# Attention scores in two full passes and packed remainders, in pairs of steps

## The reference

```python
s = (jnp.einsum('bqhd,bkhd->bhqk', q_blk[..., :QK_NOPE], k_nope)
     + jnp.einsum('bqhr,bkr->bhqk', q_blk[..., QK_NOPE:], kpe))
p = jax.nn.softmax(s.astype(jnp.float32) * scale, axis=-1).astype(v.dtype)
return jnp.einsum('bhqk,bkhd->bqhd', p, v)
```

## Time and profile before

| | us |
|---|---|
| median of three runs (3669.15 to 3674.01) | 3669.3 |
| the profiled execution, its own time | 3676.24 |
| its span, all instructions | 3674.5 |
| TensorE busy (17218 matmuls) | 3212.6, 87% |
| VectorE busy | 2016.3, 55% |
| ScalarE busy | 1054.0, 29% |
| GpSimd busy | 1035.4, 28% |

### The profile page before, as it was taken

The page is one execution under the profiler, slowest core; times in us unless marked ns, Lnnn a source line. Parts: engine busy times, 40 slices in busy tenths (PEclk is TensorE's granted clock), DMA queues, the critical chain, the costliest instruction groups (busy, mean ns, idle before and its releaser), DMA issues. The chain is left out here.

```text
span 3674.5 us, 44483 instructions
## 1 busy us (share of the span) xinstructions
PE 3212.6 (87%) x17218; PEld 2521.2 (69%) x17218; DVE 2016.3 (55%) x2246; ACT 1054.0 (29%) x1410; POOL 1035.4 (28%) x619
## 2 busy tenths in 40 slices
PE   8999999993969999999999958979982899999991
PEld 7788888871436666666666636678871789999991
DVE  2427557475357566666667644444448455555553
ACT  3411111112333333333333331212320333333332
POOL 0000000002003233333333342213320765555551
PEclk9999999995989999999999988999985899999995
DMA  4313122122230100100010025455420566666656
GB/s 169 112 39 125 57 88 99 65 99 72 71 84 20 23 5 21 23 23 5 21 23 5 6 86 166 140 194 196 140 96 27 180 195 191 189 189 189 191 162 224
DMA packets 131647, 368.44 MB, mean 100 GB/s; under 512 B 17616, under 2 KB 41952, under 8 KB 120832
## 3 DMA queue, kind: packets, MB, share of 16 engines
q1 hardware_dynamic: 89248, 259.69, 22.0%
q0 software_dynamic: 22080, 73.51, 7.2%
q10 hardware_dynamic: 20160, 33.04, 2.4%
HBM read 263.17 MB, written 102.91 MB: 100 GB/s over the span
## 5 line engine op out<-in xcount | busy, mean ns | idle before, releaser
L1057 DVE TENSOR_REDUCE at_mpart<-at_mx 128x4 f32<-128x1024 f32 (+1 forms) x291 | 352.5, 1211 | 319.1 <-PE at_mx L998 318.1
L931 ACT ACTIVATE at_w<-at_sc 128x1024 f32<-128x1024 f32 (+1 forms) x296 | 298.6, 1011 | 675.5 <-PE at_sc L978 675.5
L957 POOL TENSOR_TENSOR at_part<-at_part,at_w 128x512 f32<-128x512 f32 x224 | 291.2, 1300 | 449.4 <-ACT at_w L931 448.5
L1862 POOL TENSOR_TENSOR moe_gu_lo<-moe_raw_gu,moe_gu_hi 128x2048 fp32r<-128x2048 f32 x64 | 297.8, 4659 | 134.8 <-ACT moe_gu_hi L1901 134.4
L1010 PE MATMUL at_acc<-at_w,V 128*64 128x256 f32 (+1 forms) x2368 | 326.3, 397 | 0.0
L492 DVE SCALAR_TENSOR_TENSOR fr_r<-fr_r,fr_dw 128x2334 f32<-128x2334 f32 x120 | 318.0, 2650 | 3.9
L367 PE MATMUL fr_po<-hT_hi,fr_w_hi 128*128 128x512 f32 (+1 forms) x800 | 297.2, 371 | 2.1 <-PE fr_tp L367 1.2
L367 PE MATMUL fr_po<-hT_hi,fr_w_lo 128*128 128x512 f32 (+1 forms) x800 | 294.7, 368 | 0.0
L367 PE MATMUL fr_po<-hT_lo,fr_w_hi 128*128 128x512 f32 (+1 forms) x800 | 294.7, 368 | 0.0
L976 PE MATMUL at_sc<-at_q_hi,at_k_hi 97*128 97x512 f32 (+1 forms) x592 | 264.2, 446 | 0.0
L1979 DVE TENSOR_TENSOR moe_d_lo<-moe_raw_d,moe_d_hi 128x1024 fp32r<-128x1024 f32 x64 | 190.1, 2971 | 107.7 <-ACT moe_d_hi L1922 107.7
(11 more groups left out here) (316 smaller groups left out, 6961.0 us busy)
## 6 DMA issues: line engine op xcount, KB each, us to landing
moe_raw_gu<-w_gate_up SPq DMA_DIRECT2D x64, 1024.0 KB, 5.8
moe_raw_d<-w_down SPq DMA_DIRECT2D x64, 512.0 KB, 3.9
fr_wm<-w_ada_rows POOLq DMA_DIRECT2D x32, 512.0 KB, 4.7
gates_scratch<-fr_r ACTq DMA_DIRECT2D x64, 256.0 KB, 2.0
mx_gates<-gates_scratch SPq DMA_DIRECT2D x64, 256.0 KB, 4.0
fr_raw<-w_in SPq DMA_DIRECT2D x28, 512.0 KB, 4.4
fr_r<-x POOLq DMA_DIRECT2D x18, 512.0 KB, 4.7
op_m_raw<-mixed_scratch SPq DMA_DIRECT2D x9, 1024.0 KB, 5.9
```

What stands on the lines that cost most here:

```text
L931: act.activation(w[:, g % NW, :, 0:n], sc[:, 2 * (g % 2):2 * (g % 2) + 2, 0:n], ACT.Exp, scale=SM_SCALE).then_inc(exp_done, 1)
L957: pool.tensor_tensor(part[:, j % 2, 1, 0:n], before, w[:, g % NW, 1, 0:n], ALU.add).then_inc(add_p, 1)
L1057: dve.tensor_reduce(mpart[:, 0:q, c], max_bank(m)[:, 0:q, :], AX.X, ALU.max).then_inc(red_done, 1)
L1862: pool.tensor_tensor(gu_lo[:, slot], raw_gu[:, slot], gu_hi[:, slot].bitcast(F32), ALU.subtract).then_inc(glo_done, 1)
```

## The change

Scores. A key tile's 96 + 96 + 96 rows and the row of maxima are 289; the new layout packs them into two passes of 128 rows and 33 rows of rest. `ka`/`qa` hold hi·hi and the first 32 rows of lo·hi; `kb`/`qb` the other 64 rows of lo·hi and the first 64 of hi·lo; `kr`/`qr` the last 32 of hi·lo and the maximum row. In `kr` even key tiles lie in partitions 0 to 32 and odd ones in 64 to 96, and `qr` holds its rows twice, so that the rests of the two tiles of a step are products in two row halves of the array.

Order. Steps are taken in pairs. On TensorE: the rests of both steps (`rests`), the scores of g, the maximum products of g + 11, the scores of g + 1, the maximum products of g + 12, the values of g - 2 and of g - 1. A turn comes before the rests, or before the values with the maximum products behind them. On VectorE: reduction of g + 11, adds of g - 2 and g - 1, reduction of g + 12, splits.

Splits. Two lo instructions instead of one; those of keys move to GpSimd, ahead of its add; the rows that are needed twice are copied by DMAs from SBUF to SBUF, issued by SP behind the stores of the first and the second block. `AT` becomes 4, 6, 9, 11, 14, 16, 19, 21. The row of maxima is written twice. ScalarE takes outputs out after the odd steps only. At the start GpSimd also makes the rotary remainders of the keys, two instructions of 32 x 2560.

The diff, cut: the declarations of semaphores, the renamed operands of the maximum products and the memsets are left out.

```diff
-    AT = {3 * r + 2: r for r in range(PIECES)}
+    AT = {4 + 5 * r // 2: r for r in range(PIECES)}
...
-        q_hi = [p.sb(f"q_hi{u}", [HQ + 1, T], F32R) for u in range(2)]
-        q_lo = [p.sb(f"q_lo{u}", [HQ, T], F32R) for u in range(2)]
-        k_hi = [p.sb(f"k_hi{u}", [HQ + 1, KEYS], F32R) for u in range(2)]
-        k_lo = [p.sb(f"k_lo{u}", [HQ, KEYS], F32R) for u in range(2)]
+        qa = [p.sb(f"qa{u}", [P, T], F32R) for u in range(2)]
+        qb = [p.sb(f"qb{u}", [P, T], F32R) for u in range(2)]
+        qr = [p.sb(f"qr{u}", [NOPE + ROPE + 1, T], F32R) for u in range(2)]
+        ka = [p.sb(f"ka{u}", [P, KEYS], F32R) for u in range(2)]
+        kb = [p.sb(f"kb{u}", [P, KEYS], F32R) for u in range(2)]
+        kr = p.sb("kr", [NOPE + ROPE + 1, KEYS // 2], F32R)
...
             def _(sp):
                 def load(h):
-                    if h:
-                        sp.wait_ge(lo_piece, PIECES * (h - 1) + 4)
+                    wait(sp, klo_piece, 8 * h)
                     sp.dma_start(raw_k[0:NOPE, :], t["k"][h]).then_inc(k_ld, 16)
-                    if h:
-                        sp.wait_ge(lo_piece, PIECES * h)
+                    wait(sp, qlo_piece, 8 * h)
                     sp.dma_start(raw_q[:], t["q"][h]).then_inc(q_ld, 16)
+
+                def copy_keys(h):
+                    u = h % 2
+                    sp.wait_ge(hi_piece, PIECES * h + (4 if h else PIECES))
+                    sp.dma_start(kb[u][NOPE:P, :].bitcast(F32), ka[u][0:NOPE, :].bitcast(F32)).then_inc(copied, 16)
+
+                def copy_queries(h):
+                    u = h % 2
+                    sp.wait_ge(hi_piece, PIECES * h + PIECES)
+                    sp.dma_start(qa[u][HQ:P, :].bitcast(F32), qa[u][0:ROPE, :].bitcast(F32)).then_inc(copied, 16)
+                    sp.dma_start(qb[u][0:NOPE, :].bitcast(F32), qa[u][ROPE:HQ, :].bitcast(F32)).then_inc(copied, 16)
+                    sp.wait_ge(qlo_piece, 8 * h + 8)
+                    sp.dma_start(qr[u][NOPE:HQ, :].bitcast(F32), qr[u][0:ROPE, :].bitcast(F32)).then_inc(copied, 16)
 
...
                 load(0)
+                copy_keys(0)
+                copy_queries(0)
                 for h in range(H):
                     if h + 1 < H:
-                        if h == 0:
-                            sp.wait_ge(kpe_lo, 1)
                         load(h + 1)
                     for b in range(BH):
                         store(BH * h + b)
+                        if b == 0 and h + 1 < H:
+                            copy_keys(h + 1)
+                        if b == 1 and h + 1 < H:
...
 
                 act.wait_ge(kpe_ld, 16)
+                act.activation(ka[0][NOPE:HQ, :], raw_k[NOPE:HQ, :], ACT.Copy).then_inc(kpe_hi, 1)
                 for r in FIRST:
-                    split(0, r, slice(0, HQ))
-                act.activation(k_hi[1][NOPE:HQ, :], raw_k[NOPE:HQ, :], ACT.Copy).then_inc(kpe_hi, 1)
+                    split(0, r)
+                rope = raw_k[NOPE:HQ, :].rearrange("p (c k n) -> p c k n", k=2, n=P)
+                for k in range(2):
+                    act.activation(kr[k * NOPE:k * NOPE + ROPE, :].rearrange("p (c n) -> p c n", n=P), rope[:, :, k, :], ACT.Copy
+                                   ).then_inc(kpe_hi, 1)
+                act.activation(ka[1][NOPE:HQ, :], raw_k[NOPE:HQ, :], ACT.Copy).then_inc(kpe_hi, 1)
...
                                    ).then_inc(exp_done, 1)
+                    if g % 2:
+                        for before in (g - 3, g - 2):
+                            if before >= 0 and is_last(before):
+                                take_out(block_of(before))
                     l = g % PER
                     if l in AT and h + 1 < H:
                         split(h + 1, AT[l])
-                    if g >= 2 and is_last(g - 2):
-                        take_out(block_of(g - 2))
                 for g in (G - 2, G - 1):
                     if is_last(g):
                         take_out(block_of(g))
 
             @block.gpsimd
             def _(pool):
+                def split_keys(h, r):
+                    u, c = h % 2, cut(r)
+                    pool.wait_ge(hi_piece, PIECES * h + (r if h else FIRST.index(r)) + 1)
+                    for i, dst in enumerate((ka[u][HQ:P, c], kb[u][0:ROPE, c])):
+                        at, n = i * ROPE, 8 * h + 2 * r + i
+                        wait(pool, klo_piece, n)
+                        pool.tensor_tensor(dst, raw_k[at:at + ROPE, c], ka[u][at:at + ROPE, c].bitcast(F32), ALU.subtract
+                                           ).then_inc(klo_piece, 1)
+                    pool.wait_ge(klo_piece, n + 1)
+
+                for r in range(4):
+                    split_keys(0, r)
+                pool.wait_ge(kpe_hi, 1)
+                for u in range(2):
+                    pool.tensor_tensor(kb[u][ROPE:NOPE, :], raw_k[NOPE:HQ, :], ka[0][NOPE:HQ, :].bitcast(F32), ALU.subtract
+                                       ).then_inc(kpe_lo, 1)
+                    pool.wait_ge(kpe_lo, u + 1)
+
                 for g, (h, b, c) in enumerate(STEPS):
+                    if g % PER in AT and AT[g % PER] < 4 and h + 1 < H:
+                        wait(pool, add_p, ADDS[g])
+                        split_keys(h + 1, AT[g % PER])
                     if not joins(g):
                         continue
...
             def _(pe):
-                def scores(g):
+                def rests(g):
                     h, b, c = STEPS[g]
                     u, (tok, n) = h % 2, BLOCKS[b]
                     wait(pe, exp_done, g - 1)
                     if g == 1:
                         pe.wait_ge(red_done, LA)
                     if c == 0:
-                        pe.wait_ge(row_done, block_of(g) + 1)
+                        pe.wait_ge(row_done, 2 * block_of(g) + 2)
                         if b == 0:
-                            pe.wait_ge(lo_piece, PIECES * h + PIECES)
-                            if h == 1:
-                                pe.wait_ge(kpe_lo, 1)
+                            pe.wait_ge(klo_piece, 8 * h + 8)
+                            pe.wait_ge(qlo_piece, 8 * h + 8)
+                            pe.wait_ge(copied, 64 * h + 64)
+                            if h < 2:
+                                pe.wait_ge(kpe_hi, 3 + h)
+                                pe.wait_ge(kpe_lo, 1 + h)
+                    half = key_tiles(b, c) // 2 * P
+                    for k in range(2):
+                        rows = slice(k * NOPE, k * NOPE + ROPE + 1)
+                        pe.matmul(sc[:, 2 * (g % 2) + k, 0:n], kr[rows, half:half + P], qr[u][rows, tok:tok + n],
+                                  start=True, stop=False)
+
+                def scores(g):
+                    h, b, c = STEPS[g]
+                    u, (tok, n) = h % 2, BLOCKS[b]
                     for k in range(2):
                         keys = slice((key_tiles(b, c) + k) * P, (key_tiles(b, c) + k + 1) * P)
                         bank = sc[:, 2 * (g % 2) + k, 0:n]
-                        pe.matmul(bank, k_hi[u][:, keys], q_hi[u][:, tok:tok + n], start=True, stop=False)
-                        pe.matmul(bank, k_lo[u][:, keys], q_hi[u][0:HQ, tok:tok + n], start=False, stop=False)
-                        mm = pe.matmul(bank, k_hi[u][0:HQ, keys], q_lo[u][:, tok:tok + n], start=False, stop=True)
+                        pe.matmul(bank, ka[u][:, keys], qa[u][:, tok:tok + n], start=False, stop=False)
+                        mm = pe.matmul(bank, kb[u][:, keys], qb[u][:, tok:tok + n], start=False, stop=True)
                     mm.then_inc(s_mm, 1)
 
                 def turn_max(j):
...
-                for g in range(G):
-                    m = g + LA
-                    scores(g)
-                    if m < G and STEPS[m][2] == 0:
-                        turn_max(block_of(m) - 1)
-                        if g:
-                            values(g - 1)
-                        max_products(m)
+                for g in range(0, G, 2):
+                    if g + LA <= G and (g + LA == G or STEPS[g + LA][2] == 0):
+                        turn_max(block_of(g + LA - 1))
+                    for i in (g, g + 1):
+                        rests(i)
+                    for i in (g, g + 1):
+                        scores(i)
+                        m = i + LA
+                        if i == g and m < G:
+                            max_products(m)
+                    late = g + 1 + LA
+                    if late <= G and (late == G or STEPS[late][2] == 0):
+                        turn_max(block_of(late - 1))
+                        turned = True
                     else:
-                        if m < G:
-                            max_products(m)
-                        elif m == G:
-                            turn_max(block_of(G - 1))
-                        if g:
-                            values(g - 1)
+                        turned = False
```

(69 more changed lines are left out.)

8 lines of the change are left out of this document (6 added, 2 removed).

## The result

Before, the kernel took 3671.14 us (median of 6 runs, 3668.14 to 3674.12); with the change it takes 3689.24 (6 runs, 3682.99 to 3698.50). The ratio is 1.0051, 95% interval 1.0035 to 1.0067: slower by 18 us (half a percent), where +30 was forecast. The profiled execution took 3694.33 (span 3692.7), 18.1 above the one of before.

The account below looks back on a forecast made before the run. TensorE's own work was taken to set the pace. Blocks +39, prefetch -43, splits +24, start +14 and last pairs -4 made +30: 3706 us profiled, 3699 on the median's level; the forecast's own range was 3660 to 3740.

Parts of the forecast that it names:

- TensorE's work, 5.53 a pair: Attention phase: a pair's products and shape changes take 5.53 us against 6.16, with row halves overlapping, if nothing waits.
- The new wait, 0.63: Second maximum group of a pair, ready at 1.41, waits 0.63 us until 2.04 for the first group's reduction.
- VectorE, 6.34 as the upper bound: VectorE's adds, held up by GpSimd, end the second reduction at 6.2, so the next pair starts no earlier than 6.34.
- rival (a): VectorE gets both adds in a row: pair 6.24, turns lose 1.15 of stall each, 3629 us; chance 0.25.
- The turns, 8.8: Pairs in which the maxima turn last 8.8 us in both positions, 2.5 above the plain 6.3.
- Sums: At a block's end the sums no longer wait for the last add; their pair lasts 0.8 above 6.3.
- The prefetch, 43: Later first split lets the next head's keys land in time; all 43 us of stall gained (10 to 43).
- The start, +14: Before the first score, VectorE splits wait for the lock beside GpSimd's splits and remainders: +14 us (0 to 20).
- The last pairs, 0.65 each: The last eleven steps have no maximum groups, so each pair gains 0.65 us, -4 in all.
- blocks and splits together, 39 + 24: Longer blocks, 31.65 against 30.4 us over 32 blocks, cost +39; query and key splits cost +24.
- The splits: Query splits on VectorE delay the awaited reduction, 17 us; key splits on GpSimd cost 7; together +24 (5 to 45).

Follow-up runs that it names:

- max_first: The changed kernel with each pair's first maximum group moved ahead of the scores of its first step, except where a turn comes first: 3631.39 us, ratio 0.9894.
- same_half: The changed kernel with the rests of both key tiles taken from the same row half (output not the reference's): 3785.56 us, ratio 1.0305.
- dve_order: The changed kernel with VectorE's order per pair as reduction, add, reduction, add, TensorE's order untouched: 3633.35 us, ratio 0.9888.

## Why the prediction came out as it did

The sign, the mechanism and most terms were right; the sum was 12 us too high.

- **TensorE's work, 5.53 a pair:** right, by max_first (5.53) and same_half (+0.46). The Trainium skill (TensorEngine Tiling (Array Packing), Key Properties) says that different tiles can run matmuls in parallel; the trace agrees for tiles in two row halves (0.66 with the shape change, and 0.46 more with both in one half).
- **The new wait, 0.63, with 2.04 between the groups:** 2.05 measured, idle 0.48 in the trace and 0.75 a pair with all that hangs on it (6.28 - 5.53).
- **VectorE, 6.34 as the upper bound:** it doesn't bind. In some 55 undisturbed pairs of the trace the second reduction ends 4.0 to 5.95 after the first maximum group, median 5.05, not 6.2. GpSimd's waiting add doesn't always come between the two adds of VectorE: there rival (a) described the mechanism. More than half of them end before the 5.3 that (a) named as its condition. But the pair is 6.24 by TensorE's wait anyway, as (a) said too; it measured 6.28. (a) as a whole is out, since the turns did not lose their stalls.
- **The turns, 8.8:** most of 8.1 to 8.8. Those inside a pair take 8.7; those that begin with a pair 8.45, with a stall of 1.57 before the final maximum where 2.06 was worked out. Before the maxima behind the row it is 1.7 to 2.6. dve_order shows that this is VectorE's order. **Sums:** 7.13 for 7.1, no wait, as said.
- **The prefetch, 43:** 43.0 in the trace of the old kernel, 45 on the new one (38.5 in the total of the old kernel's five executions).
- **The start, +14:** 13.6. The Trainium skill's SBUF — State Buffer page (SBUF: two separate sides) describes the exclusive lock; the 6.01 us of a split beside GpSimd's instruction agree with it.
- **The last pairs, 0.65 each:** 4.58 to 4.61 against 5.22.
- **The size that was off is that of blocks and splits together, 39 + 24.** From the first score to the end of the phase the two profiles differ by +10; the forecast has 39 - 43 + 24 - 4 = +16 there, so these two measured 57 and not 63. Some 5 us of it are the 15 turns of 8.45 for 8.8. The other 6 of the 12 lie outside the phase and the start, where the code is the same, and within what runs differ by.
- **The splits came near in part by luck.** All pairs without a turn that are longer than their undisturbed kind are 21 us longer together. But 16 of the 21 are in thirteen pairs that ran partly at a granted clock of 0.50, as the one that starts at 1214.76 (rests 1.22 for 0.73, products 0.63 for 0.40). The forecast priced every term at the full clock; this cost is not in it, and it is not the splits' alone, since some of the thirteen follow the turns at the end of a head.
- **Slips in the working:** 32 x (31.65 - 30.4) is 40, not 39; an instruction of 2560 elements at 2.26 ns takes 5.8, not 5.9 (measured 6.01); the 5.93 of the earlier trace rows is the length of the VectorE instruction, not what it lost. None changes the result.
- **Not foreseen:** ScalarE's exponentials wait 29.6 us for VectorE's add to free a buffer. dve_order left that at 29.7 and gained 60 us, so it isn't what the turns cost; what it costs itself no run shows.

## What to carry to other kernels

Work taken off the engine that sets the pace is worth nothing if two writes of one tile move closer together than the reader between them needs: before packing, lay the reader's chain (0.67 + 1.23 + 0.14 here) against what is left between the writes, and move independent products in between. Two unrelated edits in one change can hide each other, here -43 and some +60; run each alone. In a shared order the reduction that the pacing engine waits for goes ahead of adds that nobody waits for. And look at the granted clock behind a stall before the stall is priced: here 65 us of the changed kernel's phase ran at half the clock.

## What the runs showed of the hardware

- Four products of 33 rows and 512 columns, two in each row half, take 0.66 from their start to the next product; by the forecast's estimate 0.18 of it is the change of array shape. The same four in one half take 0.46 more.
- Beside two GpSimd instructions of 2560 elements (12.02 us) two VectorE splits of about 0.75 us took 6.01 and 4.89. Beside pieces of 640 elements (7.95 us for four) a split took 1.97.
- In this phase waits of TensorE of 1.99 and 2.97 us were each followed by 6 us at a granted clock of 0.50. dve_order, with fewer such stalls, has 0.99 over the phase, the changed kernel 0.97.
